# First tile of layer 1 multiplied before the second modulation pair, four units instead of three taken tile by tile, and rounding placed ahead of the row copies on ScalarE

## The reference, cut to what matters

```python
cs = silu(c)
mod = cs @ ada_w[0] + ada_b[0]                      # 3072 values
shift, scale, gate = split(mod, 3)
h = x * (1.0 + scale) + shift                       # 256 x 1024
proj = h @ moba_w_in[0]                             # 256 x 4096: q, k, v, z
# attention, output product, layer norm; then a gated delta rule layer;
# then a block with mLSTM, neighbourhood and cross attention, and a gated FFN
```

## Time and profile before

| | |
|---|---|
| Time of 3 runs | 883.89, 884.08, 887.12 us; median 884.08 us |
| Profiled execution | span 882.9 us from first to last instruction; no time of its own is listed for it |
| Median less that span | 1.2 us |
| PE busy | 849.4 us (96%) |
| PEld, DVE, ACT, POOL busy | 782.9 us (89%), 615.8 us (70%), 481.2 us (55%), 62.0 us (7%) |
| Mean granted TensorE clock | 0.979 of full |

### The profile page before, as it was taken

The page is one execution under the profiler, slowest core; times in us unless marked ns, Lnnn a source line. Parts: engine busy times, 40 slices in busy tenths (PEclk is TensorE's granted clock), DMA queues, the critical chain, the costliest instruction groups (busy, mean ns, idle before and its releaser), DMA issues.

```text
span 882.9 us, 17620 instructions
## 1 busy us (share of the span) xinstructions
PE 849.4 (96%) x6554; PEld 782.9 (89%) x6554; DVE 615.8 (70%) x1071; ACT 481.2 (55%) x880; POOL 62.0 (7%) x65
## 2 busy tenths in 40 slices
PE   6999999899999999998999989999999999999997
PEld 3899989799999698998998778889999999999885
DVE  4497866668877755775886756555597697788643
ACT  3444665556773734575566446556745544555534
POOL 1000002100001001303000012200001020000000
PEclk9999999899998969999999999999999999999999
DMA  9899943324551521333554325434464455455531
GB/s 377 353 396 397 373 170 99 141 96 143 190 192 48 192 97 49 126 116 141 191 186 149 109 107 191 142 122 143 138 221 150 172 197 186 154 186 170 196 113 49
DMA packets 22013, 153.86 MB, mean 174 GB/s; under 512 B 2496, under 2 KB 2752, under 8 KB 3904
## 3 DMA queue, kind: packets, MB, share of 16 engines
q1 hardware_dynamic: 21168, 149.88, 46.6%
q0 software_dynamic: 784, 3.15, 1.0%
HBM read 151.97 MB, written 1.05 MB: 173 GB/s over the span
## 4 chain that ended last, share of the span: by engine, by line
PE 85%; DVE 7%; ACT 3%; DMA 3%; issue 1%; POOL 0%; SPq 0%; DVEq 0%; ACTq 0%
PE ps L387 44%; PE ps L1118 7%; PE ps L480 6%; PE ps L458 4%; PE ps L421 4%; DVE w_lo L1722 2%; PE ps L541 2%; PE ps L510 2%; PE ps L450 1%; ACT w_hi L1158 1%; PE ps L430 1%; DMA raw<-in_moba_first 1%; DMA proj<-in_ada_first 1%; PE ps L528 1%; DMA memkv<-in_ada_first 1%
## 5 line engine op out<-in xcount | busy, mean ns | idle before, releaser
L1722 DVE TENSOR_TENSOR w_lo<-raw,w_hi 128x1024 fp32r<-128x1024 f32 x230 | 284.1, 1241 | 101.8 <-ACT w_hi L1158 100.8
L1158 ACT CAST w_hi<-raw 128x1024 fp32r<-128x1024 f32 (+1 forms) x230 | 239.7, 1049 | 167.3 <-PE ps L387 62.1
L387 PE MATMUL ps<-in_hi,w_hi 128*128 128x256 f32 x1192 | 172.5, 287 | 3.3 <-DVE w_lo L1722 1.9
L387 PE MATMUL ps<-in_lo,w_hi 128*128 128x256 f32 x1192 | 167.3, 283 | 0.0
L387 PE MATMUL ps<-in_hi,w_lo 128*128 128x256 f32 x1192 | 167.2, 283 | 0.0
L387 PEld LDWEIGHTS ps<-in_hi,w_hi 128*128 128x128 f32 x1192 | 154.1, 192 | 8.6 <-DVE w_lo L1722 3.8
L387 PEld LDWEIGHTS ps<-in_hi,w_lo 128*128 128x128 f32 x1192 | 153.8, 192 | 0.0
L387 PEld LDWEIGHTS ps<-in_lo,w_hi 128*128 128x128 f32 x1192 | 153.7, 192 | 0.0
L1953 DVE SCALAR_TENSOR_TENSOR proj<-work,params,proj 128x256 f32 (+1 forms) x72 | 34.7, 482 | 9.5 <-ACT proj L1318 3.4
L421 PE MATMUL ps<-in_hi,w_hi 128*128 128x256 f32 x108 | 31.2, 320 | 6.1 <-ACT in_hi L1311 3.1
L1118 PE MATMUL ps<-w_hi,in_hi 128*128 128x512 f32 x88 | 34.2, 389 | 0.0
(11 more groups left out here) (405 smaller groups left out, 1305.3 us busy)
## 6 DMA issues: line engine op xcount, KB each, us to landing
raw<-in_mixed SPq DMA_DIRECT2D x24, 1024.0 KB, 6.9
raw<-in_ffn_up SPq DMA_DIRECT2D x22, 1024.0 KB, 4.8
raw<-in_gdn_in SPq DMA_DIRECT2D x16, 1024.0 KB, 4.8
raw<-in_w_in SPq DMA_DIRECT2D x16, 1024.0 KB, 4.9
raw<-in_merge SPq DMA_DIRECT2D x12, 1024.0 KB, 4.8
raw<-in_ffn_down SPq DMA_DIRECT2D x11, 1024.0 KB, 4.7
raw<-in_branch SPq DMA_DIRECT2D x6, 1024.0 KB, 4.7
raw<-in_moba_out SPq DMA_DIRECT2D x4, 1024.0 KB, 6.8
```

The costliest lines, as they stand in the source:

```text
L387: mm = pe.matmul(half(u, 0), w[:, u, k * P:(k + 1) * P], a[:, base + k, :], start=(n == 0 and k == 0), stop=(n == 2 and k == UNIT - 1))
L1158: act.copy(w_hi[:, u, :], src).then_inc(hi_done, 1)
L1722: dve.tensor_tensor(w_lo[:, u, :], src, w_hi[:, u, :].bitcast(F32), ALU.subtract).then_inc(lo_done, 1)
```

## The change

Three edits. `start_tile` goes over all four units, and the whole `unit(3)` behind the tiles goes away. Tile 0 moves from behind products(2) to ahead of products(1), with its wait for the weights, and the two dummy matmuls behind products(1) go. On ACT the rounding of tile k goes ahead of rows(k+1).

```diff
--- before.py
+++ after.py
@@ -578,11 +578,11 @@
 
             last = k == KT - 1
             pe.wait_ge(*after("in0_hi", k + 1))
-            for u in range(3):
+            for u in range(GROUP):
                 pe.matmul(half(u, 0), w_hi[:, u, k * P:(k + 1) * P], in_hi[:, k, :], start=(k == 0), stop=False)
                 pe.matmul(half(u, 0), w_lo[:, u, k * P:(k + 1) * P], in_hi[:, k, :], start=False, stop=False)
             pe.wait_ge(*after("in0_lo", k + 1))
-            for u in range(3):
+            for u in range(GROUP):
                 mm = pe.matmul(half(u, 0), w_hi[:, u, k * P:(k + 1) * P], in_lo[:, k, :], start=False, stop=last)
                 if last:
                     mm.then_inc(unit_done, 1)
@@ -595,12 +595,11 @@
         ada_products(0)
         ada_columns(0)
         warm(WARM)
+        pe.wait_ge(lo_done, GROUP)
+        start_tile(0)
         ada_products(1)
-        warm(2)
         ada_columns(1)
         ada_products(2)
-        pe.wait_ge(lo_done, 3)
-        start_tile(0)
         ada_columns(2)
         for p in range(3, KT):
             ada_products(p)
@@ -608,8 +607,6 @@
             ada_columns(p)
         start_tile(KT - 2)
         start_tile(KT - 1)
-        pe.wait_ge(lo_done, 4)
-        unit(3)
         project("moba_in", None, first_group=1, groups=5)
 
         def moba_values(n):
@@ -1224,10 +1221,10 @@
         for n in range(GROUP):
             high("moba_in", n)
         for k in range(KT):
+            act.wait_ge(*after("h0", k + 1))
+            act.copy(in_hi[:, k, :], first_h[:, k, :]).then_inc(sem("in0_hi"), 1)
             if k + 1 < KT:
                 copy_rows(k + 1)
-            act.wait_ge(*after("h0", k + 1))
-            act.copy(in_hi[:, k, :], first_h[:, k, :]).then_inc(sem("in0_hi"), 1)
             act.activation(x_t[:, k, :], x_t[:, k, :], ACT.Copy, scale=ALPHA).then_inc(sem("x_alpha"), 1)
         project("moba_in", plain(proj), groups=6)
```

## The result

The changed kernel takes 888.59 us (median of 20 executions, 885.10 to 892.45) against 885.62 us for the kernel before (20 executions, 879.94 to 887.82). The ratio is 1.0043 with a 95% interval of 1.0027 to 1.0059: 3.8 us slower, 2.4 to 5.2. (The ratio is the one on record; the two medians by themselves differ by 3.0 us.) So the loss is real, near 0.4%, and 1.4 us larger than the 2.4 us forecast. Single executions of one and the same kernel differ by 8 us; why is part of what follows.

A forecast was written before the change was run, and what follows sets the result against it. TensorE work laid end to end was taken as the bound. Unit 4 starting at 42.9 instead of 40.51 gives +2.4 us: span 882.9 + 2.4 = 885.3, plus 1.2 to the median, 886.5 us; range 884.4 to 889.0.

The forecast's parts named there:

- The refill of unit 4's place: Behind tile 7: with unit 3 gone, TensorE waits about 2.6 us for unit 4's low part; unit 4 starts at 42.9.
- The memset and the order: Ahead of columns(2): the memset slows h of tile 1, rounding and rows(2) follow; TensorE waits 1.7 us, columns(2) at 22.05.
- The work in the tiles: Each tile grows by three matmuls, 0.36 us, so a piece takes 2.96 instead of 2.60 us; 11.4 us from products(5) to unit 0's release.
- products(4) at 25.46, products(5) at 28.42: Two pieces of 2.96 us after products(3) at 22.5; products(5) come 0.98 us behind the 27.44 of before, without a transfer wait.
- the end of the dummy matmuls: At the start: recorded until 15.97, so tile 0 starts at 15.85 and products(1) at 17.38 instead of 16.02.
- the clock behind the wait ahead of columns(2): Start of the kernel: no clock loss was counted behind this 1.7 us wait; the pieces after it take 2.96 us.
- the clock falls in the new wait: Rival: half clock behind the 2.6 us wait ahead of unit 4 costs 1.7 us more, ending at 888.2 us; chance 0.20.
- reach the end: Behind unit 4: its shift of +2.4 us passes through to the kernel's end, giving a span of 885.3.
- 22.40 us without a gap: Behind unit 4: TensorE is busy 22.40 of 22.40 us up to 60 us, so the shift is not absorbed.
- 1.2 us from span to time: Whole kernel: 1.2 us between median and span, added to the span of 885.3 to give 886.5 us.
- not slower, or faster: Rival: the shift removes later half-clock stretches; two falling away give back 3.4 us, ending at 883.1 us; chance 0.10.

The follow-up runs named there:

- four units only: Kernel before with start_tile taking all four units and the whole unit 3 gone; tile 0, dummy matmuls and ScalarE's order stay: ratio 1.0017 to before.
- wait filled: Changed kernel with six dummy matmuls between tile 7 and unit 4, in the wait for unit 4's low part: ratio 1.0077 to before.
- order alone: Kernel before with ScalarE's rounding put ahead of the row copies and nothing else changed: ratio 1.0013 to before.
- changed again: The changed kernel itself, measured once more as a control on one chip with three other runs: ratio 1.0046 to before.
- cover back: Changed kernel with three units in the tiles and unit 3 whole behind them again: ratio 1.0055 to before.
- delay behind filled wait: Changed kernel with ten dummy matmuls ahead of unit 4, instead of the six of wait filled: ratio 1.0082 to before.
- tile 0 first only: Kernel before with three-unit tile 0 ahead of products(1), no dummy matmuls behind products(1), tile 0's rounding ahead of rows(1): ratio 1.0003 to before.
- start filled: Changed kernel with one dummy matmul behind products(1) and three behind products(2), in the waits for row copies: ratio 1.0059 to before.
- memset late: Changed kernel with GpSimd's memset released by products(3) instead of products(1): ratio 1.0038 to before.
- pure delay: Kernel before with four dummy matmuls (1.7 us) between unit 3 and unit 4, nothing else moved: ratio 1.0003 to before.
- all filled: Changed kernel with memset released by products(3), one dummy matmul each behind products(1) and products(2), six ahead of unit 4: ratio 1.0028 to before.
- cover back, memset late: Changed kernel with three units in the tiles, unit 3 whole behind them, and GpSimd's memset released by products(3): ratio 0.9994 to before.

## Why the prediction came out as it did

*The refill of unit 4's place: right.* Forecast 2.6 us of wait and 3.1 us from the last release to unit 4; measured 2.49 to 2.50 us in every kernel that leaves it open, and 3.13 us from 42.94 to 46.07. The cover of unit 3 was the right thing to look at. For its loss by itself 1.4 us were expected; "four units only" gives 1.5 us with an interval that takes in no change at all, and 1.9 us without clock.

*The memset and the order: right in mechanism and size.* columns(2) were forecast 3.12 us behind columns(1); 3.17 were measured. The wait ahead of columns(2), forecast 1.7 us, was 1.56.

*The work in the tiles: right.* A piece takes 2.96 us wherever the clock is full, and from products(5) to the release of unit 0 it took 11.29 us (forecast 11.4).

*The step that failed: "products(4) at 25.46, products(5) at 28.42".* They started at 28.49 and 31.65, the latter 3.2 us late. Two terms of the sum are wrong there.

The first is the end of the dummy matmuls, taken as 15.97 from one profile. With it products(1) started at 18.96 instead of 17.38, 1.6 us late: 1.25 us of that is the longer run of the dummy matmuls, and 0.18 us that TensorE's first matmul came later (6.32 against 6.14). The dummy matmuls run at half pace until the first rise of the clock, and that rise does not come at the same point of every execution. In the profile of before they took 6.41 us, in that of the changed kernel 7.66; over all profiles it is 6.27 to 7.70. In the run with the wait filled, with an early rise, products(1) started at 17.42, the forecast to 0.04. Before the change, the wait for the transfer ahead of products(5) can take up a late rise. In the profile of the order alone products(2) start 0.76 us later than in that of before, and products(5) only 0.46, which is what the transfer itself is later (TensorE's first matmul is 0.43 us later there as well). The change uses that wait up, and so lets a late rise through; so does "four units only".

The second is the clock behind the wait ahead of columns(2). The forecast had this wait (1.7 us) and put its effect on the clock at nothing, without a reason: its pieces of 2.96 us are at full speed. Measured were 4.26 and 3.16 us, 1.5 us more. In the five profiles with that wait unfilled the clock fell every time (changed, changed again, wait filled, cover back, delay behind filled wait). Where the memset was moved (three profiles), or only the first rounding had gone ahead of its row copy (tile 0 first only, one profile), and where the wait was filled (one profile), it did not.

*The rival "the clock falls in the new wait" was given 0.20.* It happened in three of five profiles with that wait (changed, four units only, start filled; not in changed again and memset late) and cost 1.5 us each time. It deserved about one half. It was also looked for at one place only; the earlier wait, shorter but with another idle stretch just ahead of it, was the surer one. That is the worse miss. The Trainium skill, "TensorE: Matmul & The Clock Gate", section "Why this matters for your kernels", warns of idle gaps between bursts of matmuls. The gap that it names is longer than both waits here, so its rule would have cleared the one of 2.6 us, against how the prediction used it, and the one of 1.56 us still more. The traces show half clock behind both, and here the measurement decides.

*The end: 2.4 us forecast, 3.8 measured (2.4 to 5.2).* The terms of the first 50 us as now known are larger than that: 2.4 for the waits, 0 to 1.6 for the late rise, 1.5 for the first stretch, 1.5 in about half of the executions for the second, 5 to 6 us on the mean. In the two profiles unit 4 was 5.6 and 4.9 us late, and the span only 2.6 and 4.0 us longer. What came back lies behind 163 us, in the clock's stretches of the rest. The first matmul of the same line in the kernel before, the changed one and the one with a pure delay:

```profile
163.44 3.72 PE L472 MATMUL ps<-proj,consts 128*128 128x256 f32 x16 [0.22 <-ACT proj L1188]
```

```profile
170.47 3.72 PE L472 MATMUL ps<-proj,consts 128*128 128x256 f32 x16 [0.22 <-ACT proj L1185]
```

```profile
165.23 3.72 PE L472 MATMUL ps<-proj,consts 128*128 128x256 f32 x16 [0.22 <-ACT proj L1189]
```

At this place the changed kernel is 7.0 us late (5.6 from unit 4, and 1.5 by the clock in it), the delayed one 1.8: up to here nothing is given back. From there to the end it took 719.5, 715.0 and 715.0 us; over all fourteen profiles 715.0 to 723.0. It is long where more of the rest is granted half clock: 18.7, 11.8 and 11.8 us of lost clock in these three, and over the fourteen 0.7 us of length for each microsecond of it. The prediction had said that the early shift would "reach the end", with the clock as a rival either way. By the measure without clock it does: the pure delay of 1.7 us gives +1.4, and all filled +2.6. The forecast's 22.40 us without a gap end at 60 us, though; at unit 18 there was no slack, which it did not look at. And the clock's share of the rest differs from execution to execution by more than the whole change. So the 3.8 us are not the sum of the places in the first 50 us, and that the total came within 1.4 us of the forecast while products(5) were 3.2 us off is in part luck. That the changed kernel's mean lost clock is only 0.6 us above that of the kernel before (17.6 against 17.0 over the 95 executions), with one or two more stretches at its start, while the run with the cover back has 5 us more, is left unexplained; single kernels' means of 12 executions may be off by 1 us. It stays open whether kernels whose start moves with the clock's first rise meet the later stretches unevenly.

*The baseline.* The prediction added 1.2 us from span to time, a median of three against one profile. In the profiled executions whose time is listed it is 1.8 us. And three runs of before (median 884.08) were taken for its time; twenty gave 885.62. The rival "not slower, or faster" took 2% of half clock for about 18 us of cost. That is the lost clock; at 0.69 us of time for each microsecond of it, it is 12 to 13 us.

## What to carry to other kernels

Work moved out from behind a stage into its holes is free only if the stage has holes and nothing lives under the work at its old place: look for what it covers (here the refill of a buffer, 3.0 us under 2.9 us of matmuls) before counting what it fills. A short wait of TensorE is to be priced with the clock it may cost behind it, and a pair of small edits can be harmful where each alone is not: order alone and tile 0 alone came out at +1.2 and +0.3 us, neither clearly different from no change, and together they opened the wait behind which the clock fell. When executions differ by more than the edit, compare places in the profiles and correct the times for the granted clock before believing a difference of means. And time gained at the start is gained only as far as the next place without slack.

## What the runs showed of the hardware

An idle stretch of 1.56 us of TensorE, shortly behind one of 0.49 us, was followed by half clock in five profiles of five; one of 2.50 us after a dense stretch in three of five; one of 0.49 us behind products(1) and again behind products(2) in none of the three profiles that have just these (tile 0 first only; memset late; cover back, memset late). With dummy matmuls in the wait ahead of unit 4 the clock stayed up in three profiles of three (wait filled, delay behind filled wait, all filled), though two of the five without them kept it up too; with dummy matmuls in the wait ahead of columns(2) it stayed up in the one that has them (start filled).

A GpSimd memset of 128x3072 (2.66 us) slowed VectorE's 128x256 scale and shift from 0.41 to 1.28 and 1.56 us, while a subtraction with two inputs of the same size took 0.43 us at 17.87, inside the same memset (17.19 to 19.85) in the kernel before, against 0.43 us elsewhere. With the memset moved, h of tile 1 took 0.41 us, and the later h that it met took 0.69 us (memset late) and 1.05 us (cover back, memset late).
